# One load per loop pass split by rows: the right half of the last sixteen rows in DMAs of 6, 5, 3 and 2 rows

## The chip, the core and the metric

The kernel runs on one core of a Trainium2 chip. Its time is the device time of one execution in microseconds; the runs of the kernel before have the median 1040.47 us (three runs, 1039.09 to 1041.36). A profile is one execution taken by the hardware profiler.

## The reference

One decoder layer over 256 tokens of width 1024: a norm, a combined input projection, retention heads and block attention, an output projection, and then a mixture of experts whose weights are most of what is read:

```python
def expert_block(acc, xs):
    tok, g, e = xs
    u = jnp.dot(h_pad[tok], w1[e], preferred_element_type=jnp.float32) + b1[e]
    y = jnp.dot(clamped_swiglu(u).astype(h.dtype), w2[e], preferred_element_type=jnp.float32) + b2[e]
    return acc.at[tok].add(y * g[:, None]), None
```

There are 32 experts, each token goes to four of them, and everything is float32. w1 of one expert is 1024 x 2048 (8 MiB), w2 is 1024 x 1024 (4 MiB). All 32 experts are read once: 384 MiB of the 423 MB that the kernel reads.

## The kernel before, in words

The head (norm, projection, attention, router) takes about the first 130 us. Then the experts follow as steps. Each step gathers up to 64 token rows for its expert, multiplies them with w1 (`up`, 64 matmuls at L1837), adds the bias, and, for the expert of the step before, multiplies the activations with w2 (`down`, 32 matmuls at L1860) and adds the result to the tokens' rows (`combine`, L1806). TensorE does these in a fixed order; VectorE and ScalarE do the small work between.

The weights come through a ring of 24 slots of 1 MB (`ring`), used as twelve pairs. A chunk is 2 MB and fills one pair: four chunks of w1 and two of w2 for each step. `place_in_stream` numbers the chunks, and a chunk's pair is that number modulo twelve. A chunk can be loaded when the chunk twelve places earlier has been used; TensorE counts used chunks in the semaphore `chunk_used`, and SP waits for that count before it issues the load.

SP issues all loads, in order, on one queue. In the steps PEEL to PEEL + UNROLL - 1 (6 to 17) of each of two passes (`ITERS` is 2; the passes are written out one after the other in the first round, the only one that is run where no expert has more than 64 tokens), two chunks are loaded by one DMA of 4 MB (`load_two`, L536): 128 rows, one for each partition, of 8192 numbers, 32 KB. There are 36 such loads in a pass, 72 in all. The steps before and behind these passes use 2 MB loads or smaller ones (L549, L551, L546, L547, L543). A load adds 16 to `pair_full` of its first pair when all of it is there, and TensorE waits for that before the first matmul that reads it (in `up` and `down`).

The load that the change touches is the one with j = 12, k = 4: all of w2 of the expert of step 11 of the pass, read by the down products in step 12. In the second pass it is that of step 23, read in step 24. Its left half of columns is the first chunk, its right half the second.

In the head there are loads of another shape: the biases `b1` (two DMAs, L562) and `b2` (one, L563) go as 32 rows of 4 KB to 32 partitions each; they stand between two loads of 2 MB.

Of the kernel before, what the change touches and what calls it, by code (L numbers as in the profile page):

```python
# [23 lines left out]
P = 128  # L24
# [18 lines left out]
SLOT_COLS = 2048  # L43
# [5 lines left out]
W1_CHUNKS = C // 2  # L49
# [3 lines left out]
PEEL = 6  # L53
UNROLL = 12
ITERS = (E - PEEL - 2) // UNROLL
# [8 lines left out]
TURN0_BANK = (5, 3)  # L64
CUTS = {0: (1024, 2048), 1: (2048,), 2: (2048,), 3: (2048,), 4: (1024, 2048), 5: (2048,), 8: (2048,), 10: (2048,)}
MOVED, AHEAD = 3, 3 + PAIRS
DEAL = 4
WARM_X, WARM_WIN = 26, 12
DGE_SCRATCH = 1024
# [55 lines left out]
def local_expert(i, j):  # L125

    return i * UNROLL + j
# [12 lines left out]
def place_in_stream(j, k):  # L140

    return k if j == 0 else j * STEP_CHUNKS - W2_CHUNKS + k


def pair_of(j, k):

    return place_in_stream(j, k) % PAIRS


def doubled(j, k):  # L150

    return PEEL <= j < PEEL + UNROLL
# [7 lines left out]
def cut_count(g, n):  # L160

    return sum(len(cuts) for at, cuts in CUTS.items() if at < g) + n + 1


def pair_count(r, i, j, k):

    g = place_in_stream(j, k)
    per_round = len(range(g % PAIRS, ROUND_CHUNKS - 1, PAIRS))
    if g % PAIRS in {pair_of(j, k) for j in (PEEL, PEEL + 1) for k in range(1, STEP_CHUNKS, 2)}:
        in_loop = ITERS * TURNS  # L170
        return 16 * (r * (per_round - in_loop) + (g // PAIRS + 1) - (in_loop if j >= PEEL + UNROLL else 0))
    return 16 * (r * per_round + i * TURNS + (g // PAIRS + 1))


def layer_kernel(nc, x, norm1_w, w_in, ret_norm_w, w_out, norm2_w, w_router, b_router,
# [4 lines left out]
    wout_v = w_out.rearrange("l (c p) n -> p (l c) n", p=P)  # L180
    w1_v = w1.rearrange("l e (q p s) n -> (l e) q p (s n)", p=P, s=DEAL)
    w2_v = w2.rearrange("l e (p s) n -> (l e) p (s n)", p=P)

    ctx = ExitStack()
    with ctx:
# [3 lines left out]
        def sem(name):  # L189
            return ctx.enter_context(nc.semaphore(name))  # L190
# [4 lines left out]
        def bank(b, n=1):  # L195
            return PS[:, b * BANK:(b + n) * BANK]
# [30 lines left out]
        c_at, at = {}, 0  # L227
# [3 lines left out]
        at = 0  # L231
# [3 lines left out]
        at = 0  # L235
# [10 lines left out]
        gn = c_at["expl"][:, T * RET_HEADS * 6:T * RET_HEADS * 8].rearrange("p (g s) -> p g s", s=2)  # L246
        resid_v = resid[:, :, :].rearrange("p t (q i s) -> p t q s i", q=C // DEAL, s=DEAL)

        def x_cols(t, c):

            return resid_v[:, t, c // DEAL, c % DEAL, :]
        decay = c_at["decay"].rearrange("p (h n) -> p h n", h=RET_HEADS)
# [56 lines left out]
        pair_full = [sem(f"pair_full{d}") for d in range(PAIRS)]  # L309
# [3 lines left out]
        moved_in = sem("moved_in")  # L313
        moved_end_in = sem("moved_end_in")
        ahead_in = sem("ahead_in")
        x_in = [sem(f"x_in{k}") for k in range(T + 1)]
        cst_in = sem("cst_in")
        ident_in = sem("ident_in")
# [168 lines left out]
        def _(sp):  # L487
# [26 lines left out]
            sp.dma_start(cst[:, P:], consts[:, P:KEPT_COLS]).then_inc(small_in, 16)  # L514
            for q in range(C // DEAL):
                sp.dma_start(n2w[:, DEAL * q:DEAL * (q + 1)], norm2_w[0, DEAL * q * P:DEAL * (q + 1) * P]
                             .rearrange("(p s) -> p s", s=DEAL)).then_inc(small_in, 16)
            sp.dma_start(retw, ret_norm_w.broadcast_to([P, 512])).then_inc(retw_in, 16)
# [12 lines left out]
            def load_two(i, j, k):  # L531

                e, d = local_expert(i, j), pair_of(j, k)
                dst = ring[:, 2 * d:2 * d + 4, :].rearrange("p a n -> p (a n)")
                src = w1_v[e, k // 2, :, :] if k < W1_CHUNKS else w2_v[e - 1, :, :]
                sp.dma_start(dst, src).then_inc(pair_full[d], 16)  # L536

            def load(r, i, j, k):
# [14 lines left out]
            for g in FIRST_ORDER:  # L553
# [20 lines left out]
                if g == MOVED:  # L574
                    d = pair_of(0, g)
# [14 lines left out]
            def load_ahead_rest(j, k):  # L590
                sp.wait_ge(early_used, cut_count(MOVED, 0))
                d = pair_of(j, k)
                sp.dma_start(ring[:, 2 * d, :], w2_half(j - 1, down_chunk(j, k))[:, 0:SLOT_COLS]).then_inc(pair_full[d], 16)

            def load_cut(j, k, freed):
                e, d = local_expert(0, j), pair_of(j, k)
                src = w1_half(e, k) if k < W1_CHUNKS else w2_half(e - 1, down_chunk(j, k))
                dst = ring[:, 2 * d:2 * d + 2, :].rearrange("p a n -> p (a n)")
                at = 0
                for n, cut in enumerate(CUTS[freed]):  # L600
                    sp.wait_ge(early_used, cut_count(freed, n))
                    sp.dma_start(dst[:, at:cut], src[:, at:cut]).then_inc(early_in[freed], 16)
                    at = cut
                sp.wait_ge(chunk_used, HEAD_CHUNKS + freed + 1)
                sp.dma_start(dst[:, at:], src[:, at:]).then_inc(pair_full[d], 16)

            def step_loads(r, i, j):
                for k in range(step_chunks(j)):
                    g = place_in_stream(j, k)
                    if doubled(j, k):  # L610
                        if k % 2:
                            sp.wait_ge(chunk_used, r * ROUND_CHUNKS + i * (UNROLL * STEP_CHUNKS)
                                       + (HEAD_CHUNKS + g - PAIRS + 1))
                            load_two(i, j, k - 1)
                        continue
                    if isinstance(r, int) and g == AHEAD:
                        load_ahead_rest(j, k)
                        continue
                    if isinstance(r, int) and g - PAIRS in CUTS:
                        load_cut(j, k, g - PAIRS)  # L620
                        continue
                    if g < PAIRS:
                        if isinstance(r, int):
                            continue

                        sp.wait_ge(chunk_used, r * ROUND_CHUNKS + HEAD_CHUNKS)
                    else:

                        sp.wait_ge(chunk_used, r * ROUND_CHUNKS + i * (UNROLL * STEP_CHUNKS)
                                   + (HEAD_CHUNKS + g - PAIRS + 1))  # L630
                    load(r, i, j, k)
# [750 lines left out]
        def _(pe):  # L1382
# [427 lines left out]
            def wait_early(r, g):  # L1810

                if isinstance(r, int) and g - PAIRS in CUTS and g != AHEAD:
                    pe.wait_ge(early_in[g - PAIRS], 16 * len(CUTS[g - PAIRS]))
# [40 lines left out]
            def down_part(j, k, c0, c1, aT_n, out):  # L1854

                d, h = pair_of(j, k), down_chunk(j, k)
                for c in range(c0, c1):
                    for half in range(2):
                        cols = (c % 2) * D + half * BANK
                        last = mm(out[64 * half:64 * half + 64, :], aT_n[:, c, 64 * h:64 * h + 64],  # L1860
                                  ring[:, 2 * d + c // 2, cols:cols + BANK],
                                  start=(h == 0 and c == 0), stop=(h == 1 and c == 3))
                return last

            def down(r, i, j, k):

                if not (doubled(j, k) and k % 2):
                    pe.wait_ge(pair_full[pair_of(j, k)], pair_count(r, i, j, k))
                g = place_in_stream(j, k)
                wait_early(r, g)  # L1870
                if isinstance(r, int) and g == AHEAD:
                    pe.wait_ge(ahead_in, 16)
                if isinstance(r, int) and g in CUTS:
                    down_part(j, k, 0, 2, aT, bank(5)).then_inc(early_used, 1)
                    down_part(j, k, 2, 4, aT, bank(5)).then_inc(chunk_used, 1)
                    return
                down_part(j, k, 0, 4, aT, bank(5)).then_inc(chunk_used, 1)
# [49 lines left out]
            def expert_pe(r, i, j):  # L1927
# [16 lines left out]
                if j > 0:  # L1944
                    pe.wait_ge(actT_ready, n)
                    for k in range(W1_CHUNKS, STEP_CHUNKS):
                        down(r, i, j, k)
# [94 lines left out]
```

## Time and profile before

| | us |
|---|---|
| median of three runs | 1040.47 |
| the profiled execution | 1039.17 |
| its span, first to last instruction | 1037.3 |
| TensorE busy | 1020.7 |
| VectorE busy | 245.4 |
| ScalarE busy | 126.5 |
| read from HBM | 422.78 MB, mean 409 GB/s |

A busy TensorE is not TensorE at its peak, since the ends of its matmuls are modelled. Queue q1 is the one that SP's loads use; its share is the time that its packets took, out of the span of sixteen DMA engines. Times in the rows are microseconds from the span's start. "PEld" is the weight load of TensorE, "SPq" the issuing side of SP.

### The profile page before, as it was taken

The page shows a single profiled execution, that of the slowest core. Times are in us where ns is not written, and L with a number is a line of the kernel's source. Part 1 is how long each engine was busy: PE and PEld are TensorE (multiplying, and loading weights), DVE is VectorE, ACT ScalarE, POOL GpSimd, SP SyncE. Part 2 cuts the span into 40 slices and gives each one's busy share as a digit, 9 for nine tenths or more (in the row PEclk, how much of TensorE's full clock was granted, in tenths as well). Part 3 has the DMA queues.
Part 4 walks back from the last instruction along what each step waited for, and adds up shares of the span by engine and source line. Part 5 has one row for each costly group of instructions (what it writes and reads, how often), then busy time and mean ns, then how long its engine had stood idle before and what let it go on. Part 6 is the DMA issues. An engine that isn't in the chain of part 4 may idle for free.

```text
span 1037.3 us, 11270 instructions
## 1 busy us (share of the span) xinstructions
PE 1020.7 (98%) x4880; PEld 409.8 (40%) x4880; DVE 245.4 (24%) x610; ACT 126.5 (12%) x246; POOL 0.2 (0%) x4
## 2 busy tenths in 40 slices
PE   9999999999999999999999999999999999999996
PEld 8888433333333333333333333333333333333331
DVE  5776332111111111111111111111111111111111
ACT  2433120000000000000000000000000000000002
POOL 0000000000000000000000000000000000000000
PEclk9999999999999999999999999999999999999999
DMA  9983999999999999999999999999999999999995
GB/s 324 365 337 143 418 376 425 426 428 426 434 432 426 438 429 427 435 427 429 434 429 433 430 428 437 429 428 435 426 432 433 429 430 433 428 436 420 430 421 227
DMA packets 36104, 424.64 MB, mean 409 GB/s; under 512 B 3176, under 2 KB 16112, under 8 KB 19536
## 3 DMA queue, kind: packets, MB, share of 16 engines
q1 hardware_dynamic: 35744, 423.51, 97.0%
q8 instruction: 41, 0.67, 0.3%
q10 hardware_dynamic: 304, 0.33, 0.1%
q14 instruction: 15, 0.12, 0.0%
HBM read 422.78 MB, written 1.05 MB: 409 GB/s over the span
## 4 chain that ended last, share of the span: by engine, by line
PE 90%; DMA 7%; SPq 1%; DVE 0%; another core or an unknown queue 0%; issue 0%; ACT 0%; DVEq 0%
PE PS L1837 40%; PE PS L1860 19%; DMA ring<-in_w 7%; PE PS L1442 6%; PE PS L1806 5%; PE PS L1788 5%; PE PS L1685 3%; PE PS L1645 3%; PE PS L1895 2%; PE PS L1798 2%; PE PS L1411 1%; PE PS L1780 1%; SPq L543 1%; PE PS L1388 0%; PE PS L1968 0%; PE PS L1982 0%
## 5 line engine op out<-in xcount | busy, mean ns | idle before, releaser
L1837 PE MATMUL PS<-ring,work 128*64 128x512 f32 x1976 | 433.8, 596 | 6.0 <-DMA ring<-in_w 5.5
L1837 PEld LDWEIGHTS PS<-ring,work 128*64 128x64 f32 x1976 | 139.6, 137 | 277.2 <-issue 266.5
L1860 PE MATMUL PS<-ring,work 128*64 128x512 f32 x1024 | 227.9, 596 | 0.9 <-DMA ring<-in_w 0.8
L1860 PEld LDWEIGHTS PS<-ring,work 128*64 128x64 f32 x1024 | 72.0, 137 | 153.8 <-issue 148.9
L1300 DVE TENSOR_SCALAR work<-PS 128x512 f32<-128x512 f32 x32 | 22.1, 691 | 385.4 <-PE PS L1837 385.4
L841 ACT ACTIVATE work<-work 128x512 f32<-128x512 f32 x32 | 20.2, 631 | 523.5 <-DVE work L1300 523.5
L1265 DVE TENSOR_TENSOR work<-PS,n2w 128x512 f32<-128x512 f32 x30 | 20.7, 691 | 228.5 <-PE PS L1798 228.5
L1442 PE MATMUL PS<-ring 128*128 128x256 f32 x280 | 64.5, 382 | 0.0
L1806 PE MATMUL PS<-late,work 64*128 64x512 f32 x248 | 61.9, 616 | 0.0
L1788 PE MATMUL PS<-resid,work 128*64 128x512 f32 x248 | 58.5, 592 | 0.0
L1442 PEld LDWEIGHTS PS<-ring 128*128 128x128 f32 x280 | 51.7, 190 | 7.7 <-issue 1.4
L858 ACT ACTIVATE late<-PS 128x512 f32<-128x512 f32 x30 | 17.9, 597 | 209.8 <-PE PS L1860 209.8
L1685 PE MATMUL PS<-work 32*64 32x512 f32 x256 | 35.8, 613 | 0.0
L1273 DVE COPY work<-PS 128x256 f32<-128x256 f32 x31 | 13.2, 425 | 83.1 <-PE PS L1780 83.1
L1788 PEld LDWEIGHTS PS<-resid,work 128*64 128x64 f32 x248 | 17.9, 137 | 35.3 <-issue 35.3
L1806 PEld LDWEIGHTS PS<-late,work 64*128 64x128 f32 x248 | 21.3, 186 | 19.4 <-issue 15.8
L1798 PEld LDWEIGHTS PS<-cst,work 128*128 128x128 f32 x124 | 17.3, 209 | 25.2 <-issue 25.2
L1895 PE MATMUL PS<-cst,work 128*128 128x128 f32 x128 | 23.9, 309 | 0.5
L1798 PE MATMUL PS<-cst,work 128*128 128x128 f32 x124 | 23.2, 309 | 0.0
L1304 DVE SCALAR_TENSOR_TENSOR work<-work 128x512 f32<-128x512 f32 x32 | 22.1, 692 | 3.3
L1307 DVE TENSOR_TENSOR work<-work 128x512 f32<-128x512 f32 x32 | 22.1, 692 | 1.1
L861 ACT ACTIVATE work<-PS 128x512 f32<-128x512 f32 x31 | 18.5, 598 | 27.9 <-PE PS L1895 27.9
(196 smaller groups left out, 453.2 us busy)
## 6 DMA issues: line engine op xcount, KB each, us to landing
ring<-in_w SPq DMA_DIRECT2D x72, 4096.0 KB, 34.8
ring<-in_w SPq DMA_DIRECT2D x35, 2048.0 KB, 13.5
ring<-in_w SPq DMA_DIRECT2D x22, 1024.0 KB, 8.4
ring<-in_w_in SPq DMA_DIRECT2D x11, 1024.0 KB, 12.1
ring<-in_w_out SPq DMA_DIRECT2D x4, 1024.0 KB, 11.1
ring<-in_w SPq DMA_DIRECT2D x6, 512.0 KB, 7.0
ring<-in_w_in SPq DMA_DIRECT2D x2, 512.0 KB, 5.8
work<-in_w SPq DMA_DIRECT2D x1, 768.0 KB, 8.2
```

The lines of the kernel that those rows point to most:

```text
L1300: nc.vector.tensor_scalar(g_sb, gate_bank, LIMIT, None, ALU.min).then_inc(gate_ready, 1)
L1304: nc.vector.scalar_tensor_tensor(a_sb, a_sb, 1.0, g_sb, ALU.add, ALU.mult).then_inc(glin_ready, 1)
L1307: nc.vector.tensor_tensor(a_sb, a_sb, s_sb, ALU.mult).then_inc(act_ready, 1)
L1442: last = mm(bank(b)[:, 0:WIN_COLS], tokens[:, c, :], w[:, c, :], start=(first and c == 0), stop=(c == KH - 1), skip_group_check=not first)
L1645: return mm(bank(2 + 4 * t + j), mixT(c)[:, t * P:(t + 1) * P], w[:, c % 2, j * BANK:(j + 1) * BANK], start=(c == 4), stop=(c == 3))
L1685: last = mm(bank(b0 + v)[64 * half:64 * half + 64, :], sel[v * E:(v + 1) * E, :], turned_half(b1_sb[v * E:(v + 1) * E, :], half), start=st ...
L1788: last = mm(bank(4)[64 * half:64 * half + 64, :], pick[:, t, :], resid[:, t, half_cols(half)], start=(t == 0), stop=(t == T - 1))
L1798: last = nc.tensor.transpose(bank(4)[:, c * P:(c + 1) * P], gx_v[:, c, :], ident)
L1806: last = mm(bank(2 + 4 * t + half), put[rows, t * P:(t + 1) * P], y[rows, :], start=start, stop=False, skip_group_check=True)
L1837: last = mm(bank(b0 + v)[64 * half:64 * half + 64, :], rows[:, c, :], turned_half(w[:, v * F:(v + 1) * F], half), start=(second and c == 0 ...
L1860: last = mm(out[64 * half:64 * half + 64, :], aT_n[:, c, 64 * h:64 * h + 64], ring[:, 2 * d + c // 2, cols:cols + BANK], start=(h == 0 and ...
L1895: last = nc.tensor.transpose(out[:, c * P:(c + 1) * P], a_v[:, c, :], ident)
```

## The change

The 4 MB load (j, k) = (12, 4) of each pass is issued as six DMAs. The first brings rows 0 to 111 in their full width and counts in `pair_full`, as the whole load did. The second brings the left half (4096 numbers, 16 KB) of rows 112 to 127. The other four bring the right half of these sixteen rows, 6, 5, 3 and 2 rows at a time. These five count in a new semaphore, `strip_in`, for which TensorE also waits before it reads the load. The same bytes go to the same places.

```diff
+STRIPPED = (PEEL + UNROLL // 2, W1_CHUNKS)
+STRIPS, STRIP_COL = (6, 5, 3, 2), 2 * SLOT_COLS
+STRIP_ROW = P - sum(STRIPS)
...
+def strip_count(r, i):
+
+    return 16 * (1 + len(STRIPS)) * (r * ITERS + i + 1)
...
                 src = w1_v[e, k // 2, :, :] if k < W1_CHUNKS else w2_v[e - 1, :, :]
+                if (j, k) == STRIPPED:
+                    at = STRIP_ROW
+                    sp.dma_start(dst[0:at, :], src[0:at, :]).then_inc(pair_full[d], 16)
+                    sp.dma_start(dst[at:, 0:STRIP_COL], src[at:, 0:STRIP_COL]).then_inc(strip_in, 16)
+                    for rows in STRIPS:
+                        sp.dma_start(dst[at:at + rows, STRIP_COL:], src[at:at + rows, STRIP_COL:]).then_inc(strip_in, 16)
+                        at += rows
+                    return
                 sp.dma_start(dst, src).then_inc(pair_full[d], 16)
...
                     pe.wait_ge(pair_full[pair_of(j, k)], pair_count(r, i, j, k))
+                if (j, k) == STRIPPED:
+                    pe.wait_ge(strip_in, strip_count(r, i))
                 g = place_in_stream(j, k)
```

On SP, at the loads for step 12 of the first pass, the kernel before issues (w1 twice, w2 once for each step, each behind a wait for a used chunk):

```order
L536 DMA ring<-in_w1 128x8192 [waits chunk_used] x2
L536 DMA ring<-in_w2 128x8192 [waits chunk_used]
L536 DMA ring<-in_w1 128x8192 [waits chunk_used] x2
L536 DMA ring<-in_w2 128x8192 [waits chunk_used]
L536 DMA ring<-in_w1 128x8192 [waits chunk_used] x2
```

And the changed kernel, at the same place:

```order
L553 DMA ring<-in_w2 128x8192 [waits chunk_used]
L553 DMA ring<-in_w1 128x8192 [waits chunk_used] x2
L547 DMA ring<-in_w2 112x8192 [waits chunk_used]
L548 DMA ring<-in_w2 16x4096
L550 DMA ring<-in_w2 6x4096
L550 DMA ring<-in_w2 5x4096
L550 DMA ring<-in_w2 3x4096
L550 DMA ring<-in_w2 2x4096
L553 DMA ring<-in_w1 128x8192 [waits chunk_used] x2
```

One load of w2 has become six in its place, behind the same wait; nothing before or behind it has moved.

On TensorE, at the down products of step 12, the kernel before has (bias, then the product that reads the load, then the transposes of the next step's rows):

```order
L1685 MATMUL PS<-work 64x512 [waits bsel_ready,lin_ready]
L1685 MATMUL PS<-work 64x512 x3
L1860 MATMUL PS<-ring,work 64x512 [waits pair_full2,actT_ready]
L1860 MATMUL PS<-ring,work 64x512 x15
L1798 MATMUL PS<-cst,work 128x128 [waits rows_ready]
```

And the changed kernel:

```order
L1702 MATMUL PS<-work 64x512 [waits bsel_ready,lin_ready]
L1702 MATMUL PS<-work 64x512 x3
L1877 MATMUL PS<-ring,work 64x512 [waits strip_in,pair_full2,actT_ready]
L1877 MATMUL PS<-ring,work 64x512 x15
L1815 MATMUL PS<-cst,work 128x128 [waits rows_ready]
```

The order is the same; the first matmul on the load waits for one semaphore more.

## Rows read from the trace of the kernel before

**Rows 1.** The page: busy time, and the queue of the loads.

```profile
PE 1020.7 (98%) x4880; PEld 409.8 (40%) x4880; DVE 245.4 (24%) x610; ACT 126.5 (12%) x246; POOL 0.2 (0%) x4
q1 hardware_dynamic: 35744, 423.51, 97.0%
```

**Rows 2.** Windows: us, engines' busy us (instructions), clock, DMA share, GB/s.

```profile
300.00:400.00 100.00, 99.94 (x478) 34.23 (x476) 17.19 (x37) 8.49 (x14) 0.00 (x0) 1.00 1.00 430
...
800.00:880.00 80.00, 79.95 (x384) 28.29 (x382) 13.55 (x29) 7.27 (x12) 0.00 (x0) 1.00 1.00 430
```

**Rows 3.** The chain of waits: start us, us, what.

```profile
476.75 7.02 PE PS L1860 x32
504.11 7.02 PE PS L1860 x32
...
813.95 7.02 PE PS L1860 x32
...
838.62 49.59 DMA ring<-in_w
888.25 7.09 PE PS L1837 x32
898.08 7.07 PE PS L1860 x32
927.23 7.07 PE PS L1860 x32
...
999.54 26.46 DMA ring<-in_w
```

**Rows 4.** L536, all 72, then issues and landings about the two loads changed.

```profile
L536 SPq DMA_DIRECT2D ring<-in_w x72: 327/328/328, 248.3 to 905.2; - x72
DMA to landing us min/median/max: 13.7/34.8/51.4
...
429.07 0.33 SPq L536 DMA_DIRECT2D ring<-in_w  x1
DMA to landing us min/median/max: 28.7/28.7/28.7
439.82 0.33 SPq L536 DMA_DIRECT2D ring<-in_w  x1
...
766.27 0.33 SPq L536 DMA_DIRECT2D ring<-in_w  x1
DMA to landing us min/median/max: 43.8/43.8/43.8
```

**Rows 5.** Who waited for a load, 800 to 1037 us: total us, times, longest.

```profile
PEld PS L1837 <- DMA ring<-in_w: 9.9, 6, 2.7
```

**Rows 6.** Windows of 1 us at the end.

```profile
1020.00:1021.00 1.00, 1.00 (x6) 0.30 (x4) 0.00 (x0) 0.00 (x0) 0.00 (x0) 1.00 0.65 270
1023.00:1024.00 1.00, 1.00 (x8) 0.41 (x8) 0.00 (x0) 0.00 (x0) 0.00 (x0) 1.00 0.57 221
1025.00:1026.00 1.00, 0.87 (x4) 0.00 (x0) 0.00 (x0) 0.00 (x0) 0.00 (x0) 1.00 0.25 102
1026.00:1027.00 1.00, 0.96 (x4) 0.20 (x4) 0.00 (x0) 0.00 (x0) 0.00 (x0) 1.00 0.06 25
```

**Rows 7.** The bias loads: issues, landings of L562 and L563, and windows about them.

```profile
101.76 0.83 SPq L562 DMA_DIRECT2D work<-in_b  x2
102.64 0.47 SPq L563 DMA_DIRECT2D work<-in_b  x1
DMA to landing us min/median/max: 12.2/12.2/12.2
DMA to landing us min/median/max: 12.5/12.5/12.5
113.00:115.80 2.80, 2.80 (x13) 1.60 (x12) 1.62 (x3) 0.00 (x0) 0.00 (x0) 1.00 1.07 342
115.80:121.00 5.20, 5.20 (x14) 2.33 (x13) 0.00 (x0) 0.00 (x0) 0.00 (x0) 1.00 1.02 435
```

More of the change, by code:

```diff
@@ L315, in layer_kernel @@
         ahead_in = sem("ahead_in")
+        strip_in = sem("strip_in")
         x_in = [sem(f"x_in{k}") for k in range(T + 1)]
```

## The prediction

> **What bounds the kernel now.** I read the page first, then the stretches, the chain of waits, the landings of the large loads, and last the only transfers of the trace that reach few partitions. The page shows two resources that look full: TensorE busy 98% of the span and queue q1 97% of what sixteen DMA engines can carry [rows 1]. Which one sets the end must be read by stage. From 300 to 880 us TensorE is busy all the time and the queue too, at 430 GB/s [rows 2]; a step takes TensorE 27.36 us there (the down products of two steps in a row begin at 476.75 and 504.11 [rows 3]). A step needs 12 MiB, 12.58 MB, so it eats 460 GB/s and the queue brings 430. The difference comes out of what the ring holds: a 4 MB load lands 13.7 us after its issue at first and 51.4 us at worst [rows 4]. From 838.6 on the chain of waits goes through a DMA, and steps take 29.15 us (898.08 to 927.23 [rows 3]), which is 12.58 MB / 29.15 us = 432 GB/s: the rate of the queue. TensorE's waits for loads (six before w1 products, 9.9 us in all, the longest 2.7 [rows 5]) come only there and at the end, where the last load lands at 1026.00 [rows 3]. So the end is set by bytes through the queue, from about 250 us on without a pause: a microsecond lost there for the engine that lands last is a microsecond of the total, although TensorE does not stand still when it is lost.
>
> Which engine lands last matters, since a load counts as landed when all its engines are done. After 1020 the mean busy share of the sixteen falls in steps, 0.65 at first, then 0.57, 0.25 and 0.06 [rows 6]. At 1020.5 some ten engines (0.65 x 16) work and some six have finished, 5.5 us before the last one. The engines share out the bytes equally, but do not run equally far ahead. The edit can gain something from this, if its work goes to the engines ahead.
>
> **The change, part by part.** Per loop pass one load of 4 MB is cut into six: 112 rows of 32 KB, sixteen half rows of 16 KB (left), and the sixteen right halves as 6, 5, 3 and 2 rows. It happens twice (ITERS is 2), in loads issued at 429.07 and 766.27 [rows 4].
>
> *Issue.* Five more DMAs at 0.33 us [rows 4] are 1.6 us on SP. SP's next issue is at 439.82 [rows 4], 10 us later, and the queue has 28.7 or 43.8 us of work ahead: nothing. The new wait of TensorE stands before the down products of step 12, with all later matmuls of TensorE behind it, and VectorE and ScalarE behind those. The first time the load lands at 429.07 + 28.7 = 457.8 and is wanted at 476.75, 19 us of cover; the second time at 766.27 + 43.8 = 810.1, wanted at 813.95 [rows 3], 3.9 us. A second load that is later by more than this makes TensorE wait at once, which moves the wait but adds none, since the queue sets the end in any case.
>
> *What leaves the late engines.* One engine carries 430 / 16 = 26.9 GB/s. A half row, 16,384 B, takes 0.61 us. If a DMA of n < 16 rows uses n engines, one row each, then two engines get four half rows in place of one (+1.83 us), one gets three (+1.22), two get two (+0.61), one keeps its one, and ten get none: -0.61 us. Twice: -1.2 us at most for the engine that lands last, if it is one of the ten and the two with +3.7 us are among the six that end 5 us early.
>
> The Trainium skill says of this (DMA: Bandwidth & Descriptors, "Why a DMA increments its semaphore by 16 and not by 1") that the engine count is the largest number up to 16 that divides the outer size, and that a smaller count takes the lowest-numbered engines. The rows here show no engine numbers. By that rule the split is as above; nothing in it says that the lowest-numbered engines are ahead.
>
> *The left half, sixteen rows over all engines.* The nearest rows are the bias loads, three of 128 KB onto 32 partitions each. They are issued at 101.76, then about 102.2, and 102.64, and land 12.2, 12.2 and 12.5 us later, so at 113.96, 114.4 and 115.14 [rows 7]: 0.59 us each, 222 GB/s, where 430 would take 0.30. In the stretch from 113.0 to 115.8 the DMA share is 1.07 and the rate 342 GB/s, and just behind it 435 [rows 7]: the engines are busy and move less. So sixteen engines that write into a quarter of the partitions hinder one another. With half the rows again I take half the rate, 111 GB/s: 262,144 B take 2.36 us in place of 0.61, +1.75 us. Bounds: 0 (the hindrance is absent where engines come one by one, as the steps of [rows 6] allow) and 1.75.
>
> *The 112 rows.* 7 rows of 32 KB for each engine, 7 x 1.22 = 8.5 us at the full rate. The full rate is shown only for 128 rows, a reduced one only for 32. That sixteen engines hit different places needs a pattern of rows that seven each need not keep. Bounds: +0, and +8.5 us if all of it runs at half the rate as the 32 rows do. Neither row is nearer: by size it is like 128, by its division like neither. I take the middle, +4.3.
>
> *The right half.* -0.61 us if only the engines ahead bear it; if late ones must wait for the same partitions at 111 GB/s, +1.75. I take the middle, +0.6.
>
> Sum per pass 4.3 + 1.75 + 0.6 = 6.6 us, for two passes +13.3 us. The ends are -1.2 and 2 x (8.5 + 1.75 + 1.75) = +24 us. The profiled execution takes 1039.17 us, 1.9 more than its span; with the change 1052.4. The median of the runs is 1.3 above that execution, so the forecast for the median is 1053.7, rounded 1053.5.
>
> A rule of the Trainium skill speaks against this change in the same direction: SBUF — State Buffer, "Door 1: The DMA port swizzle", gives partitions 0 to 31 as eight of sixteen ports, partitions 0 to 15 as four (104 GB/s), and says that "the only way to hit all 16 ports is one transfer spanning all 128 partitions". The bias loads agree (222 GB/s against its 218 for eight ports). By it the left half costs what I take. For seven rows per engine in a row, each engine would cross ports that others are using, and an engine held up there keeps all that is queued behind it waiting; that is the rival with the higher price below.
>
> **The rivals.**
> 1. *The balance works* (not slower). The pieces do not hinder one another, because engines reach them at different times, and the late engines just have half a row less. For it: the uneven end in [rows 6], whose six early engines have room for 3.7 us. Against it: the half rate in [rows 7], at a place where the engines had not been made to start together either. It gives 1040.5 - 1.2 = 1039.3. It decides if the loss per pass for the last engine stays under 0.61 us.
> 2. *Half rate through all 112 rows.* Speaks for it that every load of the trace with fewer rows than 128 runs at half; against it that 112 rows reach nearly all partitions. It gives 1040.5 + 24 = 1064.5.
> 3. *No hindrance, but the engines with more work are the late ones.* 2 x 1.83 = +3.7 us, 1044.1. Ten of sixteen engines are late in [rows 6], so this needs only bad luck in the numbering.
> 4. *Losses fall on engines that are ahead.* Up to some 5 us are then hidden, and the total stays at 1040.5. Against it: the long piece touches every engine.
> 5. *The small DMAs don't go to few engines.* Then the right half is spread as the left one, and costs 0 to 1.75 us per pass beside the rest. This lies inside the forecast.
>
> **How the numbers follow.** Forecast, with its own range 1045 to 1059: 0.51. Rival 2, 1059 to 1070: 0.15. Rival 3: 0.10. Rival 1: 0.16. Rival 4: 0.08. About 0.2%, 2 us, is what a measurement of this kernel can tell from no change. Slower by more than that: 0.51 + 0.15 + 0.10 = 0.76. Within: rivals 1 and 4, 0.24, less 0.04 for a gain a little larger than worked out: 0.20. Faster: 0.04. The range from 1039.5 to 1064 leaves out half of rival 1 and half of rival 2, some 0.16.
>
> **What the profile after would show.** If the forecast holds, the rate falls under 430 GB/s for 10 to 20 us about 455 and again about 800 while the DMA share stays at 1.0; the 112-row load lands several microseconds later than 28.7 and 43.8 us after its issue; TensorE's first waits for a load come before 838, at step 24; the last steps keep 29.15 us; the last landing moves by the sum. If rival 1 holds, the rate stays flat and the steps of [rows 6] fall closer together. Under rival 3 the rate stays flat too, but the fall after 1020 gets longer. I am wrong in size if the dips last less than 3 us in all, and wrong in kind if there are none. An unchanged landing of the load with a later end would point to a cost elsewhere, which I don't expect.

## The result, and the profile after

The changed kernel takes 1071.59 us (median of six runs, 1068.55 to 1072.86), the kernel before beside it 1040.2: the ratio is 1.0302, 95% interval 1.0292 to 1.0312, or +31.4 us. The direction was forecast, the size not: 1053.5 with a range to 1064. The profiled execution takes 1072.27 us, its span is 1070.5.

The page of the changed kernel: busy time, and the queue of the loads, as in [rows 1]:

```profile
PE 1026.9 (96%) x4880; PEld 413.7 (39%) x4880; DVE 245.6 (23%) x610; ACT 126.5 (12%) x246; POOL 0.2 (0%) x4
q1 hardware_dynamic: 35840, 423.51, 97.2%
```

Same work, same bytes, and the queue's share is no lower than before although the span is 33 us longer. So the DMA engines were busy for the extra time as well, and moved nothing more in it. The windows show where (columns as in [rows 2]: DMA share and GB/s last). First the kernel before, in the two stretches around the changed loads:

```profile
440.00:490.00 50.00, 49.96 (x240) 17.42 (x238) 9.68 (x22) 4.84 (x8) 0.00 (x0) 1.00 1.00 429
790.00:850.00 60.00, 59.94 (x288) 21.52 (x286) 10.36 (x23) 5.63 (x10) 0.00 (x0) 1.00 1.01 432
```

Then the changed kernel:

```profile
440.00:490.00 50.00, 49.96 (x240) 17.42 (x238) 9.68 (x22) 4.84 (x8) 0.00 (x0) 1.00 1.00 291
790.00:850.00 60.00, 42.06 (x184) 14.28 (x182) 7.51 (x15) 3.65 (x6) 0.00 (x0) 0.83 1.00 303
...
450.00:460.00 10.00, 9.98 (x49) 3.92 (x46) 0.69 (x1) 1.19 (x2) 0.00 (x0) 1.00 0.96 215
460.00:470.00 10.00, 10.00 (x48) 3.40 (x49) 1.47 (x6) 0.00 (x0) 0.00 (x0) 1.00 1.07 133
470.00:480.00 10.00, 10.00 (x52) 3.10 (x50) 2.67 (x4) 1.23 (x2) 0.00 (x0) 1.00 0.91 360
480.00:490.00 10.00, 9.98 (x50) 3.96 (x48) 2.17 (x7) 1.19 (x2) 0.00 (x0) 1.00 1.00 429
...
500.00:520.00 20.00, 19.98 (x98) 7.06 (x96) 4.84 (x11) 2.42 (x4) 0.00 (x0) 1.00 1.01 433
```

The share stays at 1.0 and the rate falls to about half and less: for some 25 us about the first load (445 to 470), and for 30 about the second (206, 223 and 149 GB/s in the three windows of 10 us from 810 on). Bytes not moved, as time at 430 GB/s: (430 - 291) / 430 x 50 = 16.2 us about the first load, (430 - 303) / 430 x 60 = 17.7 us about the second, 33.9 together, and the profiled executions differ by 1072.27 - 1039.17 = 33.1. The two dips account for it within a microsecond.

In the first dip TensorE loses nothing: 49.96 of 50 us busy, to the digit as before. Its first wait for a load comes at 521, 0.9 us in front of a product of w1; the kernel before has none until 838. The chain of waits shows when TensorE pays in earnest (start us, us, what):

```profile
571.59 48.34 DMA ring<-in_w
619.94 0.14 issue
620.07 7.09 PE PS L1877 x32
649.23 7.07 PE PS L1877 x32
678.37 7.07 PE PS L1877 x32
...
813.42 7.76 another core or an unknown queue
821.23 9.46 PE PS L1854 x32
833.43 9.99 another core or an unknown queue
843.55 8.55 PE PS L1877 x32
...
901.59 7.06 PE PS L1877 x32
930.72 7.07 PE PS L1877 x32
```

TensorE reaches the step of 29.1 us, which the queue sets, at about 620 (620.07, 649.23, 678.37) in place of 888 [rows 3]; the reserve in the ring that would have lasted until then is gone. From the second dip on there is no reserve: TensorE stands 7.8 us before a product of w1, and 10.0 us before the down products of step 24, which read the changed load. The chain does not name what these two waited for. For the second, the view of the line that issues the four small DMAs (L550) has who waited for them:

```profile
  PE PS L1877: 10.1, 1
```

The 112-row DMA of that load had landed at 773.6 + 67.3 = 840.9, and the wait ends at 833.43 + 9.99 = 843.4: the last 2.5 us of it are for the sixteen rows. Then the step is the same as in [rows 3], 29.13 us (901.59 to 930.72). The landings of the 112-row DMAs, against 28.7 and 43.8 us in [rows 4] (that load, issued at 429.2 and 773.6; below it the longest waits):

```profile
L547 SPq DMA_DIRECT2D ring<-in_w x2: 327/328/328, 429.2 to 773.6; - x2
DMA to landing us min/median/max: 42.1/54.7/67.3
```
```profile
PEld PS L1854 <- DMA ring<-in_w: 34.1, 14, 8.7
PE PS L1877 <- DMA ring<-in_w: 11.0, 3, 10.1
```

The first is 13.4 us later after its issue. The waits of [rows 5] (9.9 us before w1 products) have become 34.1.

### The profile page after: what moved, and what is told of

Same layout as the page of the kernel before. It is cut to its first block, busy times and chain, and to the rows that moved or that the text cites. A ratio compares the mean times of both kernels' runs of the same rounds, so it can differ in the third digit from the quotient of the medians.

```text
span 1070.5 us, 11280 instructions
## 1 busy us (share of the span) xinstructions
PE 1026.9 (96%) x4880; PEld 413.7 (39%) x4880; DVE 245.6 (23%) x610; ACT 126.5 (12%) x246; POOL 0.2 (0%) x4
## 4 chain that ended last, share of the span: by engine, by line
PE 83%; DMA 13%; another core or an unknown queue 3%; DVE 0%; issue 0%; ACT 0%; DVEq 0%
PE PS L1854 36%; PE PS L1877 18%; DMA ring<-in_w 13%; PE PS L1459 6%; PE PS L1823 5%; PE PS L1805 4%; PE PS L1702 3%; PE PS L1662 3%; PE PS L1914 2%; PE PS L1815 2%; PE PS L1428 1%; PE PS L1797 1%; PE PS L1405 0%; PE PS L1987 0%; PE PS L2001 0%
## 5 line engine op out<-in xcount | busy, mean ns | idle before, releaser
L1854 PE MATMUL PS<-ring,work 128*64 128x512 f32 x1976 | 438.2, 599 | 22.9 <-DMA ring<-in_w 22.4
L1854 PEld LDWEIGHTS PS<-ring,work 128*64 128x64 f32 x1976 | 139.5, 138 | 298.6 <-issue 263.8
L1877 PEld LDWEIGHTS PS<-ring,work 128*64 128x64 f32 x1024 | 76.0, 137 | 161.8 <-issue 157.8
L1823 PEld LDWEIGHTS PS<-late,work 64*128 64x128 f32 x248 | 21.2, 186 | 19.4 <-issue 15.8
## 6 DMA issues: line engine op xcount, KB each, us to landing
ring<-in_w SPq DMA_DIRECT2D x35, 2048.0 KB, 13.4
```

What stands on the lines that cost most here:

```text
L1823: last = mm(bank(2 + 4 * t + half), put[rows, t * P:(t + 1) * P], y[rows, :], start=start, stop=False, skip_group_check=True)
L1854: last = mm(bank(b0 + v)[64 * half:64 * half + 64, :], rows[:, c, :], turned_half(w[:, v * F:(v + 1) * F], half), start=(second and c == 0 ...
```

## The experiments

Each kernel ran beside the kernel before on one chip; a ratio is given with its 95% interval, and microseconds are the difference of the medians. "The load" is the 4 MB load that the change cuts, once in each pass. "Theory A" in the expectations is my account, each time the part of it that the run bears on: the queue sets the end, and time is lost where several engines write to the same or to neighbouring partitions at one time. Such partitions are called a place there, and engines are said to meet at it.

**One pass only** (`pass1`).

```diff
-                if (j, k) == STRIPPED:
+                if (j, k) == STRIPPED and isinstance(i, int) and i == 0:
```

> Only the load of the first pass is split, that of the second goes whole, as before. Theory A (the queue sets the end from 250 us on, so time lost by it in the first pass is owed at the end, although TensorE has 19 us of cover there): half of the change's 31.4 us, so 1040 + 15.7 = 1056 us. Rival (the first pass is covered, all of the loss comes from the second, where TensorE waits): 1040 us.

Measured: 1055.2 us, 1.0141 (1.0120 to 1.0163), +14.9. Half of the change, from a load that TensorE does not wait for: in its window from 440 to 490 us the rate is 296 GB/s with TensorE busy 49.96 us, and at 790 to 850 it is 429. The idea that cover in the ring makes a loss free is out; theory A stands.

**Six DMAs by columns** (`cols6`).

```diff
+                    for n in range(6):
+                        a, b = (0, 3072, 4096, 5120, 6144, 7168, 8192)[n:n + 2]
+                        sp.dma_start(dst[:, a:b], src[:, a:b]).then_inc(strip_in if n else pair_full[d], 16)
```

> The same load in six DMAs, five of them on the new semaphore, but each with all 128 rows and a part of the columns (3072, then five times 1024). Theory A (partitions that several engines write at once are the loss): within 1 us of before, 1040. Rival B (a price for each DMA, or for the second semaphore): the full 1071.

Measured: 1040.43 us, 1.0003 (0.9992 to 1.0014). Six DMAs in place of one, the second semaphore and the second wait cost nothing that can be told from noise. The loss comes with DMAs that have not all 128 rows.

**112 and 16 full rows, no small DMAs** (`rows112_16`).

```diff
+                    sp.dma_start(dst[0:at, :], src[0:at, :]).then_inc(pair_full[d], 16)
+                    sp.dma_start(dst[at:, :], src[at:, :]).then_inc(strip_in, 16)
```

> Two DMAs of full rows: 112 rows, then the last 16, both over all engines; no DMA of few rows. Theory A: 112 rows at half rate (+8.5 us per pass) and 16 rows of 32 KB at a quarter (4.9 in place of 1.2, +3.6): +24 us in two passes, 1064. Rival C (the four small DMAs, on few engines, are the loss): 1040 to 1044.

Measured: 1070.54 us, 1.0305 (1.0279 to 1.0331), +30.3. The DMAs of 6, 5, 3 and 2 rows are not what makes the kernel slow: with sixteen rows over all engines in their place it is as slow. What they cost in themselves follows in the next runs. Theory A was right in kind and 6 us short.

**The parts, by leaving out** (`only112`, `no_right`). The first loads only rows 0 to 111, the second also the left half of the last sixteen rows; the rest of the load is left out. TensorE then multiplies with whatever stands in those rows of the ring, so only the times of these two mean something. `no_right` keeps the first of the lines below; `only112` also drops TensorE's wait for `strip_in`.

```diff
-                    sp.dma_start(dst[at:, 0:STRIP_COL], src[at:, 0:STRIP_COL]).then_inc(strip_in, 16)
-                    for rows in STRIPS:
-                        sp.dma_start(dst[at:at + rows, STRIP_COL:], src[at:at + rows, STRIP_COL:]).then_inc(strip_in, 16)
-                        at += rows
```

> Rows 0 to 111 alone are loaded; the last sixteen rows of this load are left out, so 1 MB less is read in the two passes (2.4 us of the queue). Theory A, 112 rows at half rate: 2 x 8.5 - 2.4 = +14.6, 1055 us. If the 112 rows go at the full rate (rival C): 1040 - 2.4 = 1037.6.

> The changed kernel without its four small DMAs: the right half of the last sixteen rows of this load is left out (0.5 MB less in the two passes, 1.2 us of the queue). Rows 0 to 111 alone gave 1060.8. Theory A (the left half, four engines at a place, costs 2.4 us in place of 0.6): 1060.8 + 2 x 2.4 = 1065.5 us, and the four small DMAs then cost the remaining 6. Rival (the small DMAs go beside other work and are free, the left half costs all): 1071.

Measured: 1060.78 us, 1.0204 (1.0180 to 1.0227), +20.5 for 112 rows alone; 1063.28 us, 1.0226 (1.0209 to 1.0244), +23.7 with the left half. 1 MB left out is 2.4 us of the queue, so the 112 rows cost 20.5 + 2.4 = 22.9 us over what their bytes take, 11.5 per pass. The left half adds 3.2, of which 1.2 are its bytes: 1.0 per pass more than before. The four small DMAs add 31.4 - 23.7 = 7.7, of which 1.2 are bytes: 3.3 per pass. These last two are differences between comparisons. By the intervals the 2.0 us of the left half in two passes carry some 3 us, so they are not clear of nothing, and the 6.5 us of the small DMAs carry some 2.

The window that in the changed kernel runs at 133 GB/s shows the same order, here in `only112` and then in `no_right`:

```profile
460.00:470.00 10.00, 10.00 (x48) 3.41 (x48) 1.48 (x6) 0.00 (x0) 0.00 (x0) 1.00 0.98 315
460.00:470.00 10.00, 10.00 (x48) 3.41 (x49) 1.48 (x6) 0.00 (x0) 0.00 (x0) 1.00 0.94 257
```

The 112 rows alone go at about half the rate (219 GB/s from 450 to 460) and in the first pass land 37.1 us after their issue, at about 466. The fall to under a third of the rate comes only with the last sixteen rows: it is there with the small DMAs (133), and with sixteen full rows in `rows112_16` as well (151).

**Which rows meet** (`sevens`, `contig16`, `stride8`, `stride7`). In `sevens` and `stride7` the 112 rows go as seven DMAs of 16 rows and the rest as in the change; in the other two the whole load goes as eight such DMAs. The comments tell the four apart and are not in the kernels.

```diff
+                    for a in range(0, at, 16):      # sevens: neighbouring rows
+                        sp.dma_start(dst[a:a + 16, :], src[a:a + 16, :]).then_inc(strip_in if a else pair_full[d], 16)
...
+                    for a in range(7):              # stride7: engine e gets row 7e + a
+                        sp.dma_start(dst[a:at:7, :], src[a:at:7, :]).then_inc(strip_in if a else pair_full[d], 16)
...
+                    for a in range(0, P, 16):       # contig16
+                        sp.dma_start(dst[a:a + 16, :], src[a:a + 16, :]).then_inc(strip_in if a else pair_full[d], 16)
...
+                    for a in range(8):              # stride8: rows eight apart
+                        sp.dma_start(dst[a:P:8, :], src[a:P:8, :]).then_inc(strip_in if a else pair_full[d], 16)
```

> As the changed kernel, but the 112 rows go as seven DMAs of 16 neighbouring rows each, where every engine can have but one row of each sixteen. Theory A1 (the 112-row DMA deals its rows round in the same way, engine e takes e, e + 16, ...; four engines meet at every place): the same time as the changed kernel, 1071 us. Rival A2 (it gives each engine seven neighbouring rows): sixteen neighbouring rows at a time are worse, a quarter of the rate where it was half, so at least 10 us more, 1082 or above.

> The whole load as eight DMAs of 16 neighbouring rows, one row for each engine. Theory A (places shared by neighbouring rows): four engines at each place, as the 112 + 16 rows: 1070 us or more. Rival D (what counts is only that a DMA has fewer than 128 rows, so half the rate whatever the rows are): +9.7 us per pass, 1060, the same as the next kernel.

> The whole load as eight DMAs of 16 rows that stand eight apart (rows a, a + 8, ..., a + 120), one row for each engine. Theory A: two engines at each place in place of four, so half the rate for 19.4 in place of 9.7 us, +19 us in two passes, 1060, and at least 8 us under the kernel with neighbouring rows. Rival D: the same as with neighbouring rows.

> As the changed kernel, but the 112 rows go as seven DMAs of 16 rows that stand seven apart (a, a + 7, ..., a + 105), so that engine e takes row 7e + a. Theory A2 (the 112-row DMA gives each engine seven neighbouring rows; dealt in sixteens it would have cost what the seven DMAs of neighbouring rows cost, 1081): the same time as the changed kernel, 1071 us. Rival: the pieces as such (eleven DMAs more) cost, as with the neighbouring rows, 1081.

Measured: `sevens` 1080.59 us, 1.0398 (1.0377 to 1.0419); `contig16` 1078.16, 1.0378 (1.0359 to 1.0398); `stride8` 1070.81, 1.0291 (1.0269 to 1.0313); `stride7` 1074.93, 1.0342 (1.0325 to 1.0359). The same bytes in the same number of DMAs cost 7 us less when the sixteen rows stand eight apart than when they are neighbours. So which rows a DMA has matters, not only how many (rival D falls). The sizes that theory A gave were missed: it had `stride8` at 1060, 11 us too low, and at least 8 us under `contig16`, where it is 7.3. The windows of `stride8`, then those of `contig16`, show both rates:

```profile
450.00:460.00 10.00, 9.98 (x50) 4.01 (x48) 1.15 (x2) 1.61 (x3) 0.00 (x0) 1.00 0.95 196
460.00:470.00 10.00, 10.00 (x48) 3.30 (x46) 1.48 (x6) 0.00 (x0) 0.00 (x0) 1.00 1.02 213
470.00:480.00 10.00, 10.00 (x52) 3.16 (x50) 2.67 (x4) 1.23 (x2) 0.00 (x0) 1.00 0.96 390
```
```profile
450.00:460.00 10.00, 9.98 (x49) 3.89 (x46) 0.69 (x1) 1.19 (x2) 0.00 (x0) 1.00 0.96 170
460.00:470.00 10.00, 10.00 (x48) 3.52 (x50) 1.48 (x6) 0.00 (x0) 0.00 (x0) 1.00 1.00 164
470.00:480.00 10.00, 9.41 (x48) 3.04 (x46) 2.67 (x4) 1.23 (x2) 0.00 (x0) 1.00 0.90 275
```

Rows eight apart run at 213 GB/s, half of 430, as the bias loads did; neighbours at 164, under half. The Trainium skill (SBUF — State Buffer, "Door 1: The DMA port swizzle") would have sixteen rows eight apart reach eight of sixteen ports, two engines at each, and sixteen neighbours four. The 213 agrees; for the neighbours a quarter would be 108, and the trace shows more. It could do so when engines are at different DMAs at a time, but nothing here shows which engine is at which DMA.

Two things stay untested. No run has a DMA of sixteen rows that all lie at places of their own; if the account is right, it goes at the full 430 GB/s. And each cut by rows changes not only the partitions that are written at one time, but also the parts of HBM that are read at one time. That the engines meet where they write, and not where they read, is argued from the 213 GB/s above and from `cols6`, which changes the reading too and costs nothing; a load of the same HBM rows into other partitions would settle it.

`stride7` and `sevens` ask how the 112-row DMA deals its rows. Dealt in sixteens it should lose what `sevens` loses, 40.5 us, and it loses 31.4, so it is not that. With seven neighbouring rows for each engine it should be `stride7`, which loses 35.6: 4 us more, intervals just apart. The windows of `stride7` are close to those of the changed kernel (215, 133 and 360 GB/s), while `sevens` has 160, 185 and 231 there:

```profile
450.00:460.00 10.00, 9.98 (x52) 4.01 (x48) 0.98 (x2) 1.44 (x3) 0.00 (x0) 1.00 1.03 238
460.00:470.00 10.00, 10.00 (x50) 3.40 (x48) 1.48 (x6) 0.00 (x0) 0.00 (x0) 1.00 1.03 138
470.00:480.00 10.00, 10.00 (x52) 3.06 (x50) 2.67 (x4) 1.23 (x2) 0.00 (x0) 1.00 0.90 341
```

So seven neighbouring rows for each engine are the likelier dealing, and not shown.

**What is over the double time** (`stride8` against `twoloads`). `stride8` lost 30.7 us where its 8 MB at half rate cost 19.4. In `twoloads` the next load, of w1, is cut in the same way as well, and TensorE waits for its pieces too (not shown below).

```diff
+                if (j, k) == STRIPPED2:             # (13, 0)
+                    for a in range(8):
+                        sp.dma_start(dst[a:P:8, :], src[a:P:8, :]).then_inc(strip2_in if a else pair_full[d], 16)
+                    return
```

> Two 4 MB loads in a row in each pass (that of w2 and the next of w1) go as eight DMAs of 16 rows that stand eight apart; one such load per pass cost 30.7 us in two passes, where the double time of its bytes is 19.4. Theory S (the 5.6 us per pass above that are paid once, when sixteen engines that are not in step go over from shared places to their own): 30.7 + 19.4 = 50 us, 1090. Rival (each such load costs 15.3 us): 61 us, 1101.

Measured: 1088.4 us, 1.0463 (1.0442 to 1.0484), +49.0. The windows:

```profile
450.00:470.00 20.00, 19.98 (x94) 7.23 (x92) 2.17 (x7) 1.19 (x2) 0.00 (x0) 1.00 1.02 216
470.00:490.00 20.00, 17.97 (x88) 6.29 (x84) 4.84 (x11) 2.42 (x4) 0.00 (x0) 1.00 0.98 212
490.00:510.00 20.00, 18.81 (x76) 6.51 (x80) 1.72 (x3) 0.63 (x1) 0.00 (x0) 0.83 0.99 426
```

The second load adds 18.3 us in two passes, some 3 us of uncertainty on it. That fits its double time (19.4) and not the 30.7 of the first, which costs 15.3 per pass in place of 9.7. So 5.6 us per pass are paid once, for a stretch of two cut loads as for one; longer stretches were not run. Theory S said this; that these 5.6 us arise because engines that are not in step still meet while they go over to the next, whole load is argued from it, not seen.

**Half the columns** (`halfcols`).

```diff
+                    sp.dma_start(dst[:, 0:STRIP_COL], src[:, 0:STRIP_COL]).then_inc(pair_full[d], 16)
+                    sp.dma_start(dst[0:at, STRIP_COL:], src[0:at, STRIP_COL:]).then_inc(strip_in, 16)
+                    sp.dma_start(dst[at:, STRIP_COL:], src[at:, STRIP_COL:]).then_inc(strip_in, 16)
```

> Left half of the columns whole (128 rows of 16 KB), only the right half as 112 and 16 rows of 16 KB. Theory A (the price goes with the bytes that meet at shared places): half of what the 112 + 16 full rows cost, +15 us, 1055. Rival (a price per cut load, for engines that fall out of step, whatever the bytes): over 1063.

Measured: 1058.74 us, 1.0176 (1.0159 to 1.0193), +19.4, between the two (30.3 for full rows). If the price has a part b in proportion to the bytes and a part s paid once for each load, 30.3 = b + s and 19.4 = b/2 + s give b = 21.8 and s = 8.5, or 4.3 per pass. Two numbers always fit two unknowns, so this tests nothing, and by the intervals s may be anything from 4 to 13; it only agrees with the 5.6 per pass above.

**An attempt at the balance without neighbouring rows** (`low8`).

```diff
+                    at = 4 * SLOT_COLS - 1024
+                    sp.dma_start(dst[:, 0:at], src[:, 0:at]).then_inc(pair_full[d], 16)
+                    for row in range(16):
+                        a = 32 * (row // 4) + row % 4
+                        sp.dma_start(dst[a:a + 29:4, at:], src[a:a + 29:4, at:]).then_inc(strip_in, 16)
```

> An attempt at what the change may do, without neighbouring rows: the last 1024 columns (4 KB of each row) go in sixteen DMAs of 8 rows that stand four apart, each on eight engines; the rest goes as one DMA of 128 rows. Eight engines get 32 KB more in each pass, the other eight 32 KB less (1.2 us). If the eight that take DMAs of few rows are the ones ahead at the end, and the places do not stop it: -2.4 us, 1038. If the places are as full as the engines (each place gets the same bytes as before, whoever brings them): 1040. If these eight are the late ones: +2.4 us, 1043 or up to 5 with the meeting at the places.

Measured: 1047.79 us, 1.0082 (1.0061 to 1.0103), +7.7; 408 GB/s in the window from 440 to 490. No gain, and more than the 5 us allowed for late engines with meeting at the places. Why is open: this version has seventeen DMAs for the load, and `cols6` shows only six to be free. No version here beats the kernel before.

## Why the prediction was wrong in size

*What bounds the kernel*: right. `pass1` shows it best: 19 us of cover, and all of the loss paid.

*Issue, new semaphore, new wait*: right, nothing (`cols6`).

*What leaves the late engines, -0.61 us per pass*: never seen. Rival 1 needed the last engine's loss under 0.61 us per pass; it was about 15.7. That some engines end early was read from a mean share of sixteen in [rows 6], and no view here shows a single engine. Rival 3 was priced without meeting, and the rate did not stay flat; `low8` leaves open which engines are late.

*The left half, +1.75 per pass*: measured +1.0, give or take 1.5, which fits 1.75 and fits nothing as well. The sentence that the prediction quotes from the Trainium skill, of one transfer that spans all 128 partitions, stands on that page in the section "Can I just issue two DMAs to hit both halves?".

*The right half, +0.6 per pass*: measured +3.3, give or take 1. I took the middle of -0.61 and +1.75; the measured value is above both ends. That the small DMAs go into the same few partitions as the left half just before, and one after the other, I had not priced. It is a likely cause, not a tested one.

*The 112 rows, +4.3 per pass*: this is the step that failed. I bounded it by 0 and 8.5 and took the middle, since "neither row is nearer"; `only112` shows 11.5, above the upper bound. Two things were wrong. The rate: the 112 rows go at half (219 GB/s), so the 32 rows were the nearer row and 128 was no neighbour at all. Rate does not go by how many partitions a DMA reaches, since two kinds of DMA with sixteen rows run at 213 and 164. That it goes by whether sixteen engines write to places of their own at one time fits the runs in kind (`low8` cost more than it gives) but is not shown; only DMAs of 128 rows are seen at the full rate here. The bound: half rate for the load's own bytes, 8.5 us, is not the most it can cost. The 112 rows alone cost 3.0 us more, give or take 1.2, and `twoloads` and `halfcols` have a part of 4 to 6 us per pass that is paid once; where it comes from stays open. Rival 2, half rate throughout, had the right rate for the 112 rows, at 1064.5 and with a chance of 0.15. With the once-paid 5.6 us per pass added it would have said 1075.7, against 1071.6, but its other parts, 1.75 each, are not the 1.0 and 3.3 measured, so that this is near is partly luck.

*What the profile would show*: the dips about 455 and 800 with the share at 1.0, the late landing, the unchanged steps of 29.15 us and waits before 838 all came. The dips are longer than the 10 to 20 us forecast, 25 and 30. The first wait is at 521 and the steps are those of the queue from about 620 on, and not from step 24: the 16 us lost in the first pass used up the reserve of the ring.

## What to carry to other kernels

Where a queue of loads sets the end, look at the rate beside the busy share: a share of 1.0 at half the GB/s is time lost that no wait shows, and it is owed later even if the consumer is covered now. A load cut by columns into six, with all 128 rows in each piece, was free; every cut by rows tried here cost at least the double time of its bytes plus several microseconds. Before moving work to engines that end early, price the shape that the pieces must take to get there: 1.2 us at most were to be had, and 31 were paid.

## What the runs showed that I had not expected

The waits in the second dip cost TensorE its clock: the granted clock over 790 to 850 us is 0.83, and with the level of 1.2 GHz in part of it (a granted clock of 0.58 from 815 to 820, in the first of the two long waits, and 0.50 from 820 to 825) a group of 32 matmuls took 9.46 us after the wait of 7.76 and 8.55 after that of 9.99, where it takes 7.02. That should have cost no time here, since the queue stayed at a share of 1.00 and set the pace; no run separates it.

The first cut load of a stretch costs more than the next: 15.3 us per pass for one load of 4 MB, 9.2 for a second right behind it (18.3 us in two passes).
